# Second layer's attention scheduled in pairs of steps: two score steps with four passes for maxima around them, then two value pieces back to back

## What is computed

```
def one_block(args):
    qn, qr = args
    s = (jnp.einsum('bqhd,bkhd->bhqk', qn, k_nope)
         + jnp.einsum('bqhr,bkr->bhqk', qr, k_rope)).astype(jnp.float32) * scale
    p = jax.nn.softmax(s, axis=-1).astype(v.dtype)
    return jnp.einsum('bhqk,bkhd->bqhd', p, v)
```

## Time and profile before

| what | value |
|---|---|
| median of 3 runs | 4086.06 us (4082.78 to 4087.13) |
| profiled execution, first to last instruction | 4080.8 us |
| steps of the stage, first to last ACT exponent (`PT`) | 2755.7 to 3786.7 us |
| PE busy over the whole span | 3782.8 us (93%) |
| DVE, ACT, POOL busy over the whole span | 2704.1, 2073.6, 1328.2 us |

### The profile page before, as it was taken

One profiled execution on the slowest core, in us unless ns is written; L12 is line 12 of the kernel. 1 busy time (PEld: TensorE's weight loads), 2 busy tenths in 40 slices (PEclk: granted clock), 3 DMA queues, 4 the chain that ended last, 5 costly groups with the idle time before them and its releaser, 6 DMA issues. The chain is left out here.

```text
span 4080.8 us, 77608 instructions
## 1 busy us (share of the span) xinstructions
PE 3782.8 (93%) x31472; PEld 2760.1 (68%) x31472; DVE 2704.1 (66%) x5123; ACT 2073.6 (51%) x3089; POOL 1328.2 (33%) x1072
## 2 busy tenths in 40 slices
PE   6999989889888888888998999899999999999799
PEld 5777757657677777776786878775555555555477
DVE  5577678778877878887853232456777777776533
ACT  4354688768678888775433222223333333334421
POOL 3132123233555545543110000005444445445100
PEclk9999999999999999999999999999999999999899
DMA  3244223464523443444665344663323223221243
GB/s 121 83 134 155 70 89 103 130 212 140 149 79 101 123 126 110 110 128 146 197 193 192 112 165 147 222 219 86 71 58 81 58 59 90 58 61 37 96 152 109
DMA packets 421062, 487.12 MB, mean 119 GB/s; under 512 B 118752, under 2 KB 303520, under 8 KB 420448
## 3 DMA queue, kind: packets, MB, share of 16 engines
q1 hardware_dynamic: 419584, 478.70, 39.4%
q10 hardware_dynamic: 1120, 3.45, 0.2%
HBM read 321.17 MB, written 160.86 MB: 118 GB/s over the span
## 5 line engine op out<-in xcount | busy, mean ns | idle before, releaser
L150 ACT ACTIVATE PT<-psum 128x1024 f32<-128x1024 f32 x384 | 394.2, 1027 | 639.5 <-PE psum L140 638.9
L178 DVE TENSOR_REDUCE m<-psum 128x1 f32<-128x1024 f32 x384 | 468.6, 1222 | 269.1 <-PE psum L140 269.1
L140 PE MATMUL psum<-xc,wah 128*128 128x512 f32 x1600 | 530.2, 413 | 14.7 <-DVE xc L154 7.7
L154 POOL TENSOR_TENSOR part<-PT 128x1024 f32<-128x1024 f32 x144 | 341.5, 2372 | 469.1 <-DVE all L154 379.3
L140 PE MATMUL psum<-PT,V 128*64 128x512 f32 x1536 | 371.5, 605 | 0.0
L140 PEld LDWEIGHTS psum<-xc,wah 128*128 128x128 f32 x1600 | 302.6, 193 | 93.4 <-issue 21.7
L154 POOL TENSOR_TENSOR Lm<-gm,cst 64x512 f32<-64x512 f32 x192 | 262.0, 1365 | 304.3 <-DVE gm L154 163.5
L140 PE MATMUL psum<-xc,wal 128*128 128x512 f32 x800 | 318.7, 398 | 0.0
L151 ACT ACTIVATE bias<-score,cand,cols 128x2048 bf16<-128x2048 f32 (+4 forms) x155 | 244.4, 1577 | 63.9 <-DVE cand L161 61.2
L151 ACT ACTIVATE sgn<-score,cand,cols 128x1920 bf16<-128x1920 f32 (+4 forms) x155 | 227.8, 1470 | 62.0 <-DVE cand L161 58.9
L140 PE MATMUL psum<-hc,w4h 128*128 128x512 f32 x800 | 248.4, 392 | 0.0
(11 more groups left out here) (405 smaller groups left out, 9023.9 us busy)
## 6 DMA issues: line engine op xcount, KB each, us to landing
ks<-scr_keys SPq DMA_DIRECT2D x112, 512.0 KB, 4.2
raw_a<-in_w_a SPq DMA_DIRECT2D x50, 512.0 KB, 3.7
raw_w<-in_w_in SPq DMA_DIRECT2D x32, 512.0 KB, 4.7
QNh<-scr_qnh SPq DMA_DIRECT2D x48, 256.0 KB, 5.0
QRh<-scr_qrh SPq DMA_DIRECT2D x96, 128.0 KB, 4.9
QNl<-scr_qnl SPq DMA_DIRECT2D x48, 256.0 KB, 6.5
xin<-in_x SPq DMA_DIRECT2D x16, 512.0 KB, 3.5
scr_AR<-AR SPq DMA_DIRECT2D x32, 256.0 KB, 2.4
```

The lines of the kernel that those rows point to most:

```text
L140: return self.e.matmul(out, a, b, start=start, stop=stop, skip_group_check=True)
L150: return self.e.activation(out, src, f, bias=bias, scale=scale)
L154: return self.e.tensor_tensor(out, a, b, op) if self.e else self.vector(out)
L178: return self.e.tensor_reduce(out, a, AX, op, negate=negate) if self.e else self.vector(a)
```

## The change

The loop goes over steps two at a time. A pair holds four passes: one, then the scores of the even step with a pass inside, then another pass, then the scores of the odd step with a pass inside, then both value pieces of the pair before. `acc` of the last odd step and of the even step follow, then `rc` two at a time in the pairs of steps 4 and 6, and `out` at the end of the pair of step 6. `sum` stands between the even step's scores and the third pass in the pair of step 2. The instructions are the same ones, in another order; no tile or bank is added.

```
-        for g in range(NST + 8):
+        for g in range(0, NST + 2, 2):
...
-                order_5.append(("s", g))
-            many = 3 if g < 4 else 2
+            many = 6 if g < 4 else 4
             now, passes = passes[:many], passes[many:]
-            if now:
-                with_s[g] = now[0][1:]
-            order_5 += with_row(now[:many - 1])
-            if 1 < g < NST + 2:
-                order_5.append(("pv", g // 2 - 1, g % 2))
...
+            for w in range(2):
+                order_5 += with_row(now[:1])
+                if g < NST:
+                    order_5.append(("s", g + w))
+                    if now:
+                        with_s[g + w] = now[1][1:]
+                        order_5 += with_row(now[1:2])
+                now = now[2:]
+                if w == 0 and u and r == 2:
+                    order_5.append(("sum", u - 1))
+            order_5 += with_row(now)
+            if g:
+                order_5.append(("acc", g - 1))
+                order_5 += [("pv", g // 2 - 1, w) for w in range(2)]
+            if u and r == 0:
+                order_5.append(("fold", u - 1))
+            if g < NST:
+                order_5.append(("acc", g))
+            if u and r == 0:
+                order_5 += [("half", u - 1, 0), ("half", u - 1, 1)]
+            if u and r in (4, 6):
+                order_5 += [("rc", u - 1, r - 4), ("rc", u - 1, r - 3)]
+            if u and r == 6:
                 order_5.append(("out", u - 1))
```

More of the change, by code:

```diff
@@ L3137, in program @@
                     order_5.append(("gat", u))
-                order_5.append(("s", g))
-            many = 3 if g < 4 else 2
+            many = 6 if g < 4 else 4
             now, passes = passes[:many], passes[many:]
-            if now:
-                with_s[g] = now[0][1:]
-            order_5 += with_row(now[:many - 1])
-            if 1 < g < NST + 2:
-                order_5.append(("pv", g // 2 - 1, g % 2))
[L3146 to L3150, removed]
-                order_5.append(("out", u - 1))
[L3152 to L3158, removed]
+            for w in range(2):
[21 more added lines that the diff above has]
+            if u and r == 6:
+                order_5.append(("out", u - 1))
+        order_5.remove(("acc", NST - 1))
+        order_5.insert(order_5.index(("fold", NUN - 1)) + 1, ("acc", NST - 1))
+        order_5 += [("sum", NUN - 1)] + [("rc", NUN - 1, x) for x in range(4)] + [("out", NUN - 1)]
         seq_max = [k[1:] for k in firsts] + [k[1:] for k in order_5 if k[0] == "max"]
```

## The result

The changed kernel takes 4182.69 us (median of 4 runs, 4180.58 to 4184.89), the kernel before beside it 4085.6. The ratio is 1.024, 95% interval 1.0227 to 1.0252: slower by 97 us. The forecast was 4176 in a range of 4136 to 4192.

The account below looks back on a forecast made before the run. PE's own instruction sequence was taken to bound the stage; 4080.8 us span + 54.9 (third pass waits) + 35.5 (bunched DVE work) = 4171.2, plus 5.3 from span to median = 4176.5, given as 4176, range 4136 to 4192.

Parts of the forecast that it names:

- What bounds the stage: Steady part: the stage lasts as long as PE's own instructions take one behind the other; PE busy all 100 us.
- The saving of half the changes of matmul kind: Value pieces of a pair: one entry and exit instead of two, 10.28 us against 10.60, saving 0.32 us a pair.
- The third pass waits for the second's reduce: Plain pairs: shared banks 4 and 5 stall the third pass 1.03 us; net loss 67 x 0.82 = 54.9 us.
- Pairs with sum: The 22 pairs with `sum` before the third pass: no stall, 11.47 us as before, zero loss.
- Bunched work on DVE: Work behind the fourth reduce delays passes of the next pair after steps 4 and 6: 21 x (0.32 + 1.37) = 35.5 us.
- The exclusion of `out` and POOL's addition: Pair of step 6: `out` waits until POOL's addition ends at 6.53, ends at 7.1; next pair's second pass comes at 3.7.
- By shares of bandwidth: Alternative to the DVE/POOL lock: `out` about 0.6 us earlier, some 13 us over the stage.
- my rival with 5 in 100: POOL gets in between DVE's two additions in two pairs of each unit: 84 us more, 4260 us; 5 in 100.
- a sign of being wrong: Prediction is wrong if the granted clock of 2800 to 3700 us is below 1.00.
- The rival with 3 in 100: PE's clock falls to the 1.2 GHz level for a tenth of the stage: about 100 us more, 4275 us; 3 in 100.
- What I costed at nothing: First two pairs bound 2 us either way; pairs without passes 1.5 us in all; `sum` waiting for POOL 4 us of loss.
- From the span to the median: Profiled span to run median: 5.3 us added, from 4171.2 to 4176.5 us.

Follow-up runs that it names:

- the last runs: Paired kernel with evenly spaced passes and DVE's work spread: 4080.93 us; also first four steps in old order: 4079.32; also all reciprocals between reduces: 4074.64 (ratio 0.9973).
- the kernel with even distances and bunched work: Paired kernel with passes ahead of the even scores, behind 7, 14 and all 20 score pairs, `sum` next to value pieces: 4133.33 us, ratio 1.0125.
- the two runs that took it over: Even, spread paired kernel with steps 0 to 3 in the old order: 4079.32 us; the same with all reciprocals between reduces: 4074.64 us.

## Why the prediction was right, point by point

**What bounds the stage.** Right: PE alone, so a wait on PE goes into the time whole.

**The saving of half the changes of matmul kind.** Right in kind, shown by the last runs: 10.44 for a plain pair with even distances against 10.60, although its fourth pass still waits a little. The double value piece is 3.58 to 3.59 against the forecast 3.60. In the changed kernel the wait of the third pass outweighs it.

**The third pass waits for the second's reduce.** Right. 1.94 between the two in every plain pair. The term was 67 x 0.82 = 54.9; measured 67 x 0.74 = 49.6. The 2.44 that I took for the way from one pass to the next was 2.40 to 2.42 here. Two runs show the cause from both sides: taking the wait away within the pairs gives 39 us, putting it into the kernel before costs 202.

**Pairs with sum.** Right: no stall, 11.40 against 11.47 before and forecast.

**Bunched work on DVE.** Right. The term was 21 x (0.32 + 1.37) = 35.5; measured 21 x (0.30 + 1.29) = 33.4. The exclusion of `out` and POOL's addition was seen as forecast, and moving `out` alone shows that 1.2 of the 1.6 us a unit hang on it. By shares of bandwidth, which I set beside the lock, `out` would have ended about 0.6 us earlier by my estimate. POOL never got in between the two additions, my rival with 5 in 100: their row is 2.35 or 2.36 long each time.

**The clock.** Here the prediction was wrong. It gave a granted clock below 1.00 in 2800 to 3700 us as a sign of being wrong, and the clock there is 0.98. The rival with 3 in 100 came true in part: ten drops in 21 units, 10 x 1.56 = 16 us. My argument against it (a stalled stretch at clock 1.00, one idle of 1.03 a pair) looked at the plain pair and left out the pair of step 0, which by my own sum has two idle spells 2 us apart. The Trainium skill, TensorE: Matmul & The Clock Gate, section "A second HAM failure mode: psum-queue depth-cycling", reports a kernel whose frequent short idles between groups made the clock swing. Ten of the 21 pairs of step 0 agree with that. The kernel with the wait put in does not, which idles 0.87 us in each step of 6.41 at 1.00, and nor do the first steps of the kernel before, with idle spells of 0.87 and 1.32 us 2.06 apart at 1.00.

**What I costed at nothing.** The first steps were wrong beyond the bound of 2 us. The pair of step 4 begins at 2787.36 where the step before began at 2780.90: 6.5 us. About 3.1 of them lie ahead of the first matmul of the changed loop (2757.20 against 2754.12), where nothing was changed and the granted clock from 2700 us on was 0.94 against 0.97 in the two profiled runs. The rest, 3.4, is in the first two pairs, at a mean clock of 0.89 against 1.00. Two pass intervals there are 2.54 and 4.27 us, where the same intervals are 2.06 and 2.40 at full clock, which makes 2.3 of the 3.4:

```profile
2757.00:2787.40 30.40, 22.76 (x146) 14.24 (x146) 15.99 (x14) 8.32 (x9) 20.49 (x8) 0.89 0.60 148
```

**From the span to the median.** I added 5.3 us, the distance of the median from the profiled span. The profiled execution after took 4184.89 us by its own run time with a span of 4183.1, so only 1.8 lie around the span. If as much lay around the span before, the profiled execution was the fastest of its three (4082.78), and 3.5 of the 5.3 us should not have been added. That, the two terms that were too large (7.4 us together) and the pairs with `sum` (1.5) made up for about half of the 16 us of clock and the 6.5 at the start. That the median lies within 7 us of the forecast is therefore in part luck: 22.5 us that I had at nothing stand against 12.4 that I had too many.

The sum over the profiled spans: 49.6 + 33.4 + 16 + 6.5 - 1.5 (22 pairs with `sum`, 0.07 each) = 104, and 4183.1 - 4080.8 = 102.3 were measured.

What stays open is why the granted clock falls in every second pair of step 0 and not in those between, which have the same idle spells, why it does not fall in the kernel with even distances and bunched work, whose one wait is longer, and what the first four steps cost by themselves. From the loop's first matmul to the pair of step 4 the six traces with pairs from the start take 29.9 to 35.2 us, the kernel before 26.8.

## What to carry to other kernels

Where passes share one buffer, what counts is the distance from the start of one to the start of the next against producer plus consumer (here 0.66 + 1.23 + 0.05 = 1.94 us); four passes "among" twenty score pairs are not evenly spaced if two stand on either side of a step's boundary. Merging pieces to save a change of matmul kind is worth 0.16 us a pair here, net of the little wait that is left, and it takes away the long piece that gave the second engine its time, so the small work of that engine must be laid between its urgent instructions in the same edit. An instruction that may have to wait for another engine's operation belongs behind the urgent one.

## What the runs showed of the hardware

Single idle spells of 0.87 us on PE in each 6.4 us left the granted clock at 1.00; two spells (0.99 and 0.86) about 2 us apart were followed by a stretch at 0.50 in 10 of 21 units, and moving one DVE instruction, which took away one of the two, ended all ten. A single wait of 1.69 us, in the kernel with even distances and bunched DVE work, did not bring a drop. In the first steps of the kernel before, two spells (0.87 and 1.32 us) 2.06 us apart left the clock at 1.00, while the same PE order of these steps had two stretches at 0.50 in the first of the two runs that took it over and none in the second. So neither the length of an idle spell nor the order of the instructions alone decided it here.
